# Paged attention and the first four tiles of two recurrences woven into one program, one recurrence after the other in three shared banks

## The reference, cut to what matters

```python
cols = rmsnorm(x, norm_mix) @ w_in
a_cols, b_cols, c_cols = split(cols)             # three groups of heads
o_a = gated_delta_rule(conv(a_cols), S_a)        # 6 heads of 64, chunks of 64 rows, state S[k,v]
o_b = softmax attention with two maps per head   # prompt: causal; the 8 sequences: paged
o_c = rwkv7(c_cols, S_c)                         # 6 heads of 64, state S[v,k]
x = x + concat(o_a, o_b, o_c) @ w_out
x = x + memory attention; x = x + conv ffn       # then a last norm

# o_b of the 8 sequences: each has 64 pages of 128 rows, found through a table
kp = k_pool[page_table]; vp = v_pool[page_table]        # 8 x 8192 rows of 256 floats each
s = concat(q @ kp.T, mask(q @ k_new.T)) * DB**-0.5
w = softmax(s[map 0]) - lam * softmax(s[map 1])
o_b = w[..., :past] @ vp + w[..., past:] @ v_new
```

## Time and profile before

| | us |
|---|---|
| median of 3 runs (6254.03 to 6260.93) | 6257.78 |
| the profiled execution | 6261.2 |
| its span | 6259.5 |
| PE busy | 5382.4 (86%) |
| DVE busy | 2373.1 (38%) |
| ACT busy | 1505.6 (24%) |
| POOL busy | 852.1 (14%) |

### The profile page before, as it was taken

How to read it: one execution, slowest core, us unless ns; L and a number is a source line. 1 busy time by engine, 2 the same in 40 slices (tenths; PEclk the granted TensorE clock), 3 DMA queues, 4 the chain that set the end, 5 groups by cost and what they waited for, 6 DMA issues and landing times. The chain is left out here.

```text
span 6259.5 us, 91453 instructions
## 1 busy us (share of the span) xinstructions
PE 5382.4 (86%) x35012; PEld 3324.9 (53%) x35012; DVE 2373.1 (38%) x5477; ACT 1505.6 (24%) x3427; POOL 852.1 (14%) x1191
## 2 busy tenths in 40 slices
PE   8988899976554666679999989999999989998998
PEld 5544455543332564266556565556555565565554
DVE  1166655522221455403433353433433343431322
ACT  3245543321111221002221221212212222211211
POOL 0012211113444111001100110001100011000000
PEclk9989999987776676569999989999899989999999
DMA  3111111136776101022222312222222312223232
GB/s 97 39 34 32 33 33 34 34 93 193 229 227 170 33 17 72 19 91 60 75 77 81 109 41 75 83 75 81 66 76 83 98 40 81 75 71 88 77 94 72
DMA packets 719603, 494.53 MB, mean 79 GB/s; under 512 B 78458, under 2 KB 688378, under 8 KB 719135
## 3 DMA queue, kind: packets, MB, share of 16 engines
q1 hardware_dynamic: 680193, 400.25, 22.3%
q0 software_dynamic: 24576, 67.14, 3.8%
q10 hardware_dynamic: 14400, 21.31, 0.9%
HBM read 439.38 MB, written 49.19 MB: 78 GB/s over the span
## 5 line engine op out<-in xcount | busy, mean ns | idle before, releaser
L3499 PE MATMUL s_f_b<-s_f_h,s_f_W 128*128 128x416 f32 x4480 | 1639.1, 522 | 28.8 <-DMA s_f_h<-o_t 19.7
L3499 PEld LDWEIGHTS s_f_b<-s_f_h,s_f_W 128*128 128x128 f32 x4480 | 845.1, 192 | 704.8 <-issue 687.3
L3557 PE MATMUL s_f_b<-s_f_a,s_f_W 128*128 128x416 f32 x1760 | 634.1, 516 | 0.2
L537 PE MATMUL s_p_acc<-s_hT,s_p_W 128*128 128x416 f32 x1600 | 625.9, 538 | 6.3 <-DMA s_p_W<-in_w_in_dram 6.3
L3557 PEld LDWEIGHTS s_f_b<-s_f_a,s_f_W 128*128 128x128 f32 x1760 | 328.5, 190 | 263.5 <-issue 257.4
L537 PEld LDWEIGHTS s_p_acc<-s_hT,s_p_W 128*128 128x128 f32 x1600 | 299.4, 196 | 285.1 <-issue 269.0
L1332 POOL DMA_DIRECT2D s_V<-in_cache_diff_v_dram x512 | 274.8, 537 | 400.4 <-issue 398.6
L3758 DVE TENSOR_TENSOR s_f_xT<-s_f_xT,s_f_b 128x416 f32<-128x416 f32 x160 | 93.5, 586 | 587.3 <-PE s_f_b L3557 533.3
L3779 POOL TENSOR_TENSOR s_f_ex<-s_f_ex,s_f_mix 128x416 f32<-128x416 f32 x105 | 111.7, 1064 | 1306.4 <-ACT s_f_mix L3585 1305.8
L1098 ACT ACTIVATE s_prob<-s_s_ps,s_ntop 128x512 f32<-128x512 f32 (+3 forms) x320 | 196.5, 619 | 368.9 <-DVE s_ntop L1149 368.8
L1356 PE MATMUL s_tp<-s_ident,s_K 128*128 128x128 f32 x1024 | 164.2, 315 | 119.0 <-DMA s_K<-in_cache_diff_k_dram 116.4
(11 more groups left out here) (687 smaller groups left out, 8212.3 us busy)
## 6 DMA issues: line engine op xcount, KB each, us to landing
s_f_W<-in_ffn_w_in_dram SPq DMA_DIRECT2D x220, 512.0 KB, 3.9
s_K<-in_cache_diff_k_dram SPq DMA_DIRECT2D x512, 128.0 KB, 2.9
s_V<-in_cache_diff_v_dram POOLq DMA_DIRECT2D x512, 128.0 KB, 3.1
s_f_W<-in_ffn_w_out_dram SPq DMA_DIRECT2D x80, 448.0 KB, 3.8
cols_t<-s_p_out ACTq DMA_DIRECT2D x100, 208.0 KB, 1.9
s_f_W<-in_w_out_dram SPq DMA_DIRECT2D x40, 512.0 KB, 4.6
s_f_W<-in_ffn_w_out_dram SPq DMA_DIRECT2D x40, 512.0 KB, 4.1
s_r_c<-cols_t SPq DMA_DIRECT2D x16, 704.0 KB, 6.9
```

Source lines behind the costliest of these rows:

```text
L537: mm = pe.matmul(self.acc[n % 2][:, 0:CH], self.W[:, u, k, :], self.hT[:, k, c * CH:(c + 1) * CH], start=(k == 0), stop=(k == KD - 1))
L3499: mm = pe.matmul(bank(u)[:, 0:G], w[:, k, :], h[:, k, :], start=(k == 0), stop=(k == KD - 1 and kind != "op"))
L3557: mm = pe.matmul(bank(u)[:, 0:G], w[:, k, :], a[:, f % NA, :], start=(k == 0), stop=(k == len(part) - 1))
```

## The change

`diff_paged` becomes `paged_lanes`, with the same work in the same order per engine, cut in 162 slots (one a step, and one at each end). The delta rule's four tiles (96 slots) and then RWKV's four (100 slots) are made one lane of 196 slots, which is woven with the paged one. Both recurrences get the same three banks and, one after the other, the same on-chip memory, so every engine waits between them until the delta rule's last store is done and RWKV's constants are in. The paged lane has two `tp` banks (3 before), K buffers for 6 groups (8) and V buffers for 7 (8). The list of small loads is split: some go with `front`, 46 into the woven stage, six and one into the sample stage. Indentation aside, the core of the diff is:

```diff
-def diff_paged(nc, pr, C, later):
-    KG, VG, NT = 8, 8, 3
+def paged_lanes(nc, st, pr, C):
+    KG, VG, NT = 6, 7, 2
+    L = Lanes()
+    L.slots = 16 * (NB + 2) + 2
...
+    applied = lambda a: 16 * (a // 4 + 1) + (5, 8, 11, 14)[a % 4]
+    v_slot, at = {}, 1
+    for g in range(G):
+        at = max(at + 1, applied((g - VG) // 4) + 1 if g >= VG else 0)
+        v_slot[at] = g
...
+    def sp_lane(sp):
+        def k_pages(g):
             if g >= KG:
                 sp.wait_ge(flipped, place[("k", g - KG, 1)] + 1)
             for i in range(4):
+                sp.dma_start(K[:, g % KG, i, :], kp[page_of(sp, g, i)]...).then_inc(k_in[g % KG], 16)
         sp.dma_start(table[:, :], ...).then_inc(init, 16)
         sp.wait_ge(init, 16)
+        for g in range(KG):
+            k_pages(g)
+        yield
+        for s in range(16 * (NB + 2)):
+            if 1 <= s <= G - KG:
+                k_pages(s + KG - 1)
+            yield
...
+    def pool_lane(pool):
...
+        for s in range(16 * (NB + 2)):
+            if s in v_slot:
+                g = v_slot[s]
                 if g >= VG:
                     pool.wait_ge(pv, (g - VG) // 4 + 1)
                 for i in range(4):
+                    pool.dma_start(V_[:, g % VG, i, :], vp[page_of(pool, g, i)]...)\
+                        .then_inc(v_in[g % VG], 16)
+            yield
...
+class Shared:                       # hands out the same banks again; memory of its own, freed at exit
...
+def in_turn(eng, one, done, two):
+    yield from one
+    for sem, n in done:
+        eng.wait_ge(sem, n)
+    yield from two
```

In `build` (the first lines are the block that now stands ahead of the woven stage):

```diff
+                with Stage(nc) as es:
+                            for r in two:
+                                sp.dma_start(C.levels[r, :, :], ins["c_levels"][0:HD, 0:6, 0:HD]).then_inc(arrived, 16)
+                            sp.wait_ge(arrived, 32)
+                            dve.memset(S_g[:, :, :], 0.0)
+                            dve.memset(S_r[:, :, :], 0.0)
...
-                diff_paged(nc, pr, A_, loads)
...
-                with Stage(nc) as ls:
-                    D_ = gdn_lanes(nc, ls, pr, S_g, C, 0, LEAD)
-                    R_ = rwkv_lanes(nc, ls, pr, S_r, C, 0, LEAD)
+                with Stage(nc) as ps:
+                    K_ = paged_lanes(nc, ps, pr, A_)
+                    banks = [ps.ps(f"shared{j}", [P, 512]) for j in range(3)]
+                    with Shared(ps, banks) as gs:
+                        D_ = gdn_lanes(nc, gs, pr, S_g, C, 0, LEAD)
+                    with Shared(ps, banks) as rs_:
+                        R_ = rwkv_lanes(nc, rs_, pr, S_r, C, 0, LEAD)
+                    done = ((D_.stored, 16 * LEAD), (r_in, 16 * len(r_loads)))
+                    both = lambda eng, one, two: (in_turn(eng, one(eng), done, two(eng)), n_slots)
+                    def states(sp):
+                        for dst, src in r_loads:              # 17
+                            sp.dma_start(dst, src).then_inc(r_in, 16)
+                        for dst, src in loads:                # 29, one a slot
+                            sp.dma_start(dst, src).then_inc(loads_in, 16)
+                            yield
...
-                            weave((D_.pool(pool), D_.slots), (R_.pool(pool), R_.slots))
+                            weave((K_.pool(pool), K_.slots), both(pool, D_.pool, R_.pool))
```

```diff
+                    if t >= 2:
+                        act.wait_ge(turned, 2 * t - 2)
-                    act.activation(sq[0:n, :], x[0:n, t % 3, :], ACT.Square, accum_out=ss[0:n, u:u + 1])\
+                    act.activation(xn[0:n, u, :], x[0:n, t % 3, :], ACT.Square, accum_out=ss[0:n, u:u + 1])\
...
-                    if t >= 2:
-                        act.wait_ge(turned, 2 * t - 2)
```

More of the change, by code:

```diff
@@ new lines, in paged_lanes @@
+    squared, logged, rooted, normed, stored = (
+        st.sem(x) for x in ("squared", "logged", "rooted", "normed", "stored"))
+    plan = {3: "top", 4: "t0", 5: "p0 t1", 6: "mB t2", 7: "t3", 8: "p1 D t4", 11: "p2", 14: "p3"}
+    flip_order, cross_order = [], []
+    for b in range(NB + 2):
+        for k in range(16):
+            if k == 0 and b >= 2:
+                cross_order += [("fin", b - 2)]
+            if b < NB:
+                flip_order += [("k", 16 * b + k, 0), ("k", 16 * b + k, 1)]
+            if 1 <= b <= NB:
+                here = plan.get(k, "").split()
+                flip_order += [("t", b - 1, int(x[1])) for x in here if x in ("t0", "t1", "t2", "t3", "t4")]
+                cross_order += [(x, b - 1) for x in here if x in ("top", "mB", "D")]
+            if k == 12 and b < NB:
+                cross_order += [("new", b)]
@@ new lines, in pe_lane @@
+                    flip_k(16 * b + k)
+                if k % 4 == 1 and 0 < 16 * b + k - 1 <= G:
+                    score((16 * b + k - 1) // 4 - 1)
+                for x in plan.get(k, "").split() if 1 <= b <= NB else []:
+                    if x == "top":
+                        top_row(b - 1)
+                    elif x == "mB":
+                        top_back(b - 1)
+                    elif x == "D":
+                        denominators(b - 1)
+                    elif x[0] == "t":
+                        flip_p(b - 1, int(x[1]))
+                    else:
+                        apply(b - 1, int(x[1]))
@@ new lines, in paged_lanes, with __init__, __enter__, __exit__ @@
+    L.sp, L.pe, L.act, L.dve, L.pool = sp_lane, pe_lane, act_lane, dve_lane, pool_lane
+    return L
+class Shared:
+    def __init__(self, st, banks):
+        self.st, self.banks, self.mem = st, iter(banks), Stage(st.nc)
+        self.sem, self.steps = st.sem, st.steps
+    def __enter__(self):
+        self.mem.__enter__()
+        self.sb = self.mem.sb
+        return self
+    def __exit__(self, *a):
+        return self.mem.__exit__(*a)
+    def ps(self, name, shape):
+        return next(self.banks)
@@ L3853, in build @@
+            for r in (slice(0, HD), slice(HD, P)):
+                later += [(C.eye[r, :], ins["c_ident"][0:HD, 0:HD]),
+                          (C.incl[r, :], ins["c_incl"][0:HD, 0:HD]), (C.strict[r, :], ins["c_strict"][0:HD, 0:HD])]
             with Stage(nc) as fs:
@@ L3955, in build @@
+                r_loads = [(w2a2[0:64, :], ins["rw_w2"][0]), (w2a2[64:P, :], ins["rw_a2"][0]), (g2[:, :], ins["rw_g2"][0]),
+                           (lnw[:, :], row(ins["rw_lnx_w"], P)), (lnb[:, :], row(ins["rw_lnx_b"], P))]
+                r_loads += [(C.mask2[r, m, a * HD:(a + 1) * HD], ins["c_mask2p"][0:HD, a * P:a * P + HD])
+                            for r in two for m in range(3) for a in range(2)]
                 C.f_taps, C.f_bias = sb("f_taps", [P, FB, 3]), sb("f_bias", [P, FB])
@@ L4036, in build @@
                     w_in = {n: wst.sem(n + "_in") for n in w_of}
+                    f_in = wst.sem("f_in")
                     def ahead(sp):
+                        with nc.allow_non_contiguous_dma("small vectors to columns"):
+                            for dst, src in f_loads:
+                                sp.dma_start(dst, src).then_inc(f_in, 16)
                         for n in w_of:
```

800 lines of the change are left out of this document (387 added, 413 removed).

## The result

The kernel after takes 6034.91 us, median of 3 runs (6032.44 to 6050.77), against 6257.78 (6254.03 to 6260.93): a ratio of 0.9651, 95% interval 0.9624 to 0.9678. The forecast was 6025, its range 5950 to 6150. The profiled execution took 6032.4 us (6028 in the forecast's sum) with a span of 6030.6, which is 228.9 less than before.

| stretch, us | before | after | forecast |
|---|---|---|---|
| prompt's last store to the table load | 5.0 | 9.8 | +3 |
| table load (1348.1, 1349.7) to RWKV's fourth store | 1091.4 | 865.4 | -237 |
| of it: to the first apply | 106 | 125 | 118 |
| first apply to the last V page | 571 | 673 | 676 |
| last V page to that store | | 67 | 60 |

What follows compares the result with a forecast made beforehand. POOL's V-page issue bounds from the first apply on, SP's K pages before. Terms 118 + 576 + 52 + 36 + 12 + 60 = 854 us against 1091; -237 + 4 = -233 gives 6025 us, range 5950 to 6150.

Steps and rivals of the forecast that it cites:

- First apply, 118 us: Start of the woven stage: SP brings 88 K pages and 17 small loads before PE's first apply; ends 106 and 130.
- V pages, 576 us: POOL's queue after the first apply: 484 remaining V pages at 1.19 us each, 576 us.
- POOL's recurrence work, 52 us: POOL's delta-rule and RWKV instructions, standing in the same queue as the V pages: 52 us.
- POOL's waits, 36: POOL waiting for recurrence inputs among its V pages: 6 us for each of six tiles, ends 0 and 72.
- the switch, 12: From delta rule to RWKV: a store, then a load of RWKV's first tile; 12 us, ends 5 and 20.
- The chains alone, 548 us: Both recurrences without paged work: about 4 x (65 + 72) = 548 us, used in rivals 2 and 3.
- the 60 us of the last slots: Woven stage's last 22 recurrence slots, with no paged work beside them: 60 us, between 35 and 88.
- Rival 2: Woven stage: the recurrence chain becomes the bound; 1074 us with nothing hidden, half the excess 964, time 6135; chance 0.17.
- Rival 3: Woven stage: paged steps and chains run one after the other; 1234 us, time 6405, decides from 1087; chance 0.04.
- (1), POOL without waits: Woven stage: drift between queues takes all of POOL's waits; stage 801 us, time 5972; chance 0.20.
- (4), the port: DVE locks POOL's descriptor port: all pages at the longer issue, +97 us, time 6122 (24 on a quarter); chance 0.06.
- Edges: Around the woven stage: +3 for the block ahead, +1 for the flips, nothing for the other loads; +4 in all.

Runs made afterwards that it cites:

- e1: Kernel after with V pages taken in pool order, no table look-up of V; 5966.3 us.
- e2: Kernel after with K pages taken in pool order, no table look-up of K; 6019.7 us.
- e10: Kernel after with POOL's recurrence slots two slots later among its V pages, other engines' orders unchanged; 6008.0 us.
- e3: Kernel after with neither K nor V pages looked up in the table; 5918.2 us.
- e6: Kernel after with the recurrences' 196 slots placed over the first 0.92 of the paged lane's length on every engine; 6036.0 us.
- e8: Kernel after with one register load of four page numbers per group of four V pages on POOL; 5995.5 us.
- e9: Kernel after with one register load of four page numbers per group, for K on SP and V on POOL; 5967.4 us.
- e4: Kernel after with all paged slots ahead of the recurrences' slots on every engine, in place of woven; 6524.3 us.

## Why the prediction was right, point by point

*The bound.* POOL's page queue from the first apply on, K before it: right, by e1, e2 and e10. One reading on the way was too large: the 400 us of "issue" are not all spent on loading page numbers. 70 of them are one wait, with all buffers full, for the first apply:

```profile
1457.55 0.54 POOL L1332 DMA_DIRECT2D s_V<-in_cache_diff_v_dram  x1 [69.86 <-issue]
```

The forecast does not rest on it, since its page term is counted from the first apply on.

*First apply, 118 us:* measured 125, inside its ends. Of the 19 us over before, 17 are SP's: the 88th K page, the last that this apply needs, was issued 99.6 us after the table load before and 116.8 after. SP's timeline:

```profile
1354.22 30.85 SPq L1322 DMA_DIRECT2D s_K<-in_cache_diff_k_dram  x28
1385.11 0.52 SPq L4081 DMA_DIRECT2D s_w2a<-in_rw_w_dram  x1
...
1387.88 8.30 SPq L4081 DMA_DIRECT2D s_mask<-in_c_mask2p_dram  x12
...
1397.58 3.67 SPq L1322 DMA_DIRECT2D s_K<-in_cache_diff_k_dram  x4
1401.37 0.39 SPq L3064 DMA_DIRECT2D s_g_cq<-cols_t  x1
```

The 17 constants are 11 us, as I had. The first K page comes 4.6 us after the table load for 2.3 before, and the rest, 4 us, are the second tile's two loads and three more small ones, for which I had 1 us. With the constants spread the page came at 107.4 and the apply at 116. One thing that looks like a cause is none: PE's first matmul of the stage starts at 1360.09, 10.4 us after the table load, because POOL's three memsets for the paged lane, and DVE's copies after them, stand behind the delta rule's first POOL slot. In run e10 those memsets go first and PE starts 7.4 us after the table load, and the first apply comes at 126 all the same.

*V pages, 576 us:* measured 563, the 15 us of waits for applies included. A page cost 1.16 us and not 1.19. After a recurrence instruction the next page's number is already loaded: up to three pages follow at 0.56 us, as in POOL's timeline of the kernel after:

```profile
1702.33 1.00 POOL L2579 TENSOR_TENSOR s_g_gB<-s_g_AP,s_levels 128x384 f32<-128x384 f32 x1
1703.28 1.00 POOL L2579 TENSOR_TENSOR s_g_Eb<-s_g_AP,s_levels 128x384 f32<-128x384 f32 x1
1704.21 1.68 POOL L1351 DMA_DIRECT2D s_V<-in_cache_diff_v_dram  x3
```

*POOL's recurrence work, 52 us:* measured 50.

*POOL's waits, 36, and the switch, 12:* together 48, measured 62. Of the terms of this stretch it is the one that is off by the most, and still inside its ends. I took 12 us a tile from the waits for E and let a drift of the queues halve it. The largest wait is one that the earlier trace rows did not show: RWKV's first level mask behind its front slots (30 us in three tiles, the longest, 17.4, in the tile after the switch, in which DVE waited 9.3 us for the tile's load). From the delta rule's last store, 1782.05, to RWKV's first load, 1787.02, it is 5 us. Drift took up little. The chains alone are nearly as long as POOL's queue, so POOL is not late everywhere; that follows from the next point.

*The chains alone, 548 us:* measured 631. It entered the rivals and, by the 60 us of the last slots (measured 67), the sum. What failed there was to add up durations at the clock of a stage where two chains shared PE. Rival 2 with the measured chains, 631 + 364 + 162 = 1157, lies further from the result of 865 than with mine. Run e3, with no look-up left, puts all of the paged work and the chains into 745 us, 114 above the chains alone, at a granted clock of 0.84. Rival 3's serial stage is 1353 us where I had 1234; both are far above the point of 1087 from which it decides.

*The sum* of the stretch came out at 676 for 673 because the page term was 13 us too high, the recurrences' work 2 too high and the waits 14 too low. The agreement is better than the terms, and so far luck.

*PE at 74% of 854 us:* measured 68% of 865, since its work shrank from 632 to 591 us as the clock rose. I had said that it should rise and not let it into the number.

*Rivals.* (1), POOL without waits: out as it stands, but run e10, with 18 us of waits for 62, came 27 us nearer to it. (4), the port: the mean of all V pages is 540 ns for 537, median 536 at both. The one page of 0.73 us that I put down to DVE's copies is the first V page, and the first takes 0.73 us in run e10 as well, where it starts at 1361.47 and DVE's copies have ended at 1361.45:

```profile
1361.47 0.73 POOL L1351 DMA_DIRECT2D s_V<-in_cache_diff_v_dram  x1 [0.69 <-issue]
```

So the +97 us had no ground, nor the 24. The rule of the Trainium skill, SBUF — State Buffer, section "SBUF: two separate sides", that DVE can lock POOL out of the port, does not show here: with 203 us of DVE work laid beside it the queue lost nothing. As few of these instructions are copies from on-chip to on-chip memory, no run tests it either.

*Edges.* From the stage's last store to the last stage's first load it is 2 us more, for 1. The block ahead of it cost 4.9 us, for +3; the working there was wrong, since the gap of 6 us that I set against the block's 9 lies inside the 1091 us and was subtracted twice. Two loads and a barrier were cheaper than 9. Counted once, the gap would have put the forecast at 6031. The last stage, whose program is only shifted, took 3446.4 us after and 3452.3 before, counted from its first load of `s_f_h`, but this is no gain of the change: with the code of the kernel after it also took 3452 in the profiles of e6, e8 and e9. So 6 of the 228.9 us are a difference between executions that went the forecast's way; what makes it is open. The prompt's stage ended 3.3 us sooner in the profile of after, but in e1 to e4, which share its code, at 1343.6 to 1344.5 for 1343.1 before: that is such a difference too.

## What to carry to other kernels

When a lane is woven in beside a queue that is the bound, try the other lane's slots not where their input is expected but some slots later: an engine that waits in order makes everything behind it wait, and two slots on POOL alone were worth 27 us here. Measure a chain alone before pricing it: taken out of company this one ran at a granted clock of 0.55 in place of 0.70, and took 631 us where I had 548. Look at more than one profile before giving a few us to the change: the same last stage took 3445 to 3452 us. And before hiding a queue of issues behind other work, look at what is idle in front of each issue; one load of four numbers took off 129 us with no weave at all.

## What was not expected of the hardware

- A look-up of one number costs POOL 0.60 us in front of a page, of four numbers 1.35 us; the load instruction in it takes 0.29 us with one and 0.33 with four, and the work on each number 0.17.
- These look-ups run ahead under POOL's own compute instructions: behind two masks of 1.0 us, three pages went out in 1.68 us.
- With no look-up, eight V pages went out in 4.27 us (run e1, 1704.23 us), 0.53 each.
- One chain alone, PE 56% busy in 661 us (36 of them before its first matmul), was granted 0.55 of the clock; two chains together, 67% busy in 400 us, 0.70; one chain with paged attention, 71% busy in 673 us, 0.83.
